# Layer 1's modulation summed on VectorE in layer 0's feed-forward, and the two context units of a head pair apart in layer 1's latent attention

## What is computed

```python
mod = jax.nn.silu(cond) @ lp["w_mod"] + lp["b_mod"]            # (1024) @ (1024, 6144), for 2 conditions
sh1, sc1, g1, sh2, sc2, g2 = jnp.split(mod[:, None, :], 6, axis=-1)
h = _rms(x, lp["norm1_g"]) * (1.0 + sc1) + sh1
z = h @ lp["w_in"]                                             # queries, keys, values and gates of three branches
...
o_a = _attend(q_a, k_a, v_a)                                   # branch B, latent attention, 8 heads
o_d = _attend(q_d0, k_d0, v_all, q_d1, k_d1, lam)              # branch D, differential attention, 4 heads
x = x + g1 * (y @ lp["w_out"])
h2 = _rms(x, lp["norm2_g"]) * (1.0 + sc2) + sh2
x = x + g2 * (jnp.square(jax.nn.relu(h2 @ lp["w_ff1"])) @ lp["w_ff2"])
```

## Time and profile before

| | |
|---|---|
| median of 3 runs | 2543.97 us |
| the profiled execution | 2543.29 us, span 2541.5 us |
| TensorE busy | 2466.6 us (97% of the span) |
| VectorE busy | 1115.3 us (44%) |
| ScalarE busy | 827.5 us (33%) |
| GpSimd busy | 1347.6 us (53%) |
| mean granted TensorE clock | 0.994 of full speed |

### The profile page before, as it was taken

How to read it: one execution, slowest core, us unless ns; L and a number is a source line. 1 busy time by engine, 2 the same in 40 slices (tenths; PEclk the granted TensorE clock), 3 DMA queues, 4 the chain that set the end, 5 groups by cost and what they waited for, 6 DMA issues and landing times.

```text
span 2541.5 us, 41382 instructions
## 1 busy us (share of the span) xinstructions
PE 2466.6 (97%) x17104; PEld 2314.0 (91%) x17104; DVE 1115.3 (44%) x1610; ACT 827.5 (33%) x1517; POOL 1347.6 (53%) x635
## 2 busy tenths in 40 slices
PE   5999999999999999999989999999999999999997
PEld 3989976988999999999979899679889999999997
DVE  5443465434446423132564525653454463222235
ACT  3261355435422302021224423553554132112031
POOL 2646520554566666666656456016455666666664
PEclk8999999999999999999999999999999999999999
DMA  6202235521122222222211122342111222222221
GB/s 270 75 26 76 78 112 181 195 86 50 51 70 73 75 75 75 75 75 75 75 58 59 39 80 78 142 158 79 55 42 62 72 75 75 75 76 75 75 75 58
DMA packets 62619, 214.63 MB, mean 84 GB/s; under 512 B 6816, under 2 KB 11360, under 8 KB 62176
## 3 DMA queue, kind: packets, MB, share of 16 engines
q1 hardware_dynamic: 56160, 202.92, 23.9%
q10 hardware_dynamic: 6272, 9.07, 1.0%
HBM read 207.14 MB, written 4.49 MB: 83 GB/s over the span
## 4 chain that ended last, share of the span: by engine, by line
PE 90%; DVE 4%; ACT 2%; DVEq 1%; issue 1%; DMA 1%; SPq 1%; POOL 0%; POOLq 0%; ACTq 0%
PE big L567 22%; PE big L571 22%; PE big L570 22%; PE four L753 6%; PE big L828 2%; PE big L776 2%; PE four L649 2%; PE four L859 2%; PE four L840 2%; PE four L798 1%; PE big L595 1%; PE big L598 1%; PE big L599 1%; PE four L973 1%; DMA first_mod<-in_first 1%
## 5 line engine op out<-in xcount | busy, mean ns | idle before, releaser
L527 POOL TENSOR_TENSOR w_hi<-raw,cst 128x1024 fp32r<-128x1024 f32 (+1 forms) x286 | 546.4, 1910 | 1044.3 <-PE big L567 835.2
L530 POOL TENSOR_TENSOR w_lo<-raw,w_hi 128x1024 fp32r<-128x1024 f32 (+1 forms) x286 | 734.5, 2568 | 40.8
L567 PE MATMUL big<-act_hi,w_hi 128*128 128x320 f32 x2304 | 716.8, 311 | 1.3 <-DVE act_lo L2214 1.2
L571 PE MATMUL big<-act_hi,w_lo 128*128 128x320 f32 x2304 | 711.8, 309 | 0.0
L570 PE MATMUL big<-act_lo,w_hi 128*128 128x320 f32 x2304 | 711.8, 309 | 0.0
L567 PEld LDWEIGHTS big<-act_hi,w_hi 128*128 128x128 f32 x2304 | 432.5, 188 | 8.9 <-issue 5.6
L570 PEld LDWEIGHTS big<-act_lo,w_hi 128*128 128x128 f32 x2304 | 432.5, 188 | 1.1
L571 PEld LDWEIGHTS big<-act_hi,w_lo 128*128 128x128 f32 x2304 | 432.4, 188 | 0.0
L567 PE MATMUL big<-u_hi,w_hi 128*128 128x320 f32 (+1 forms) x1024 | 319.0, 312 | 1.9 <-DVE u_lo L2233 1.9
L570 PE MATMUL big<-u_lo,w_hi 128*128 128x320 f32 (+1 forms) x1024 | 317.4, 310 | 0.0
L571 PE MATMUL big<-u_hi,w_lo 128*128 128x320 f32 (+1 forms) x1024 | 317.0, 310 | 0.0
(11 more groups left out here) (328 smaller groups left out, 4040.6 us busy)
## 6 DMA issues: line engine op xcount, KB each, us to landing
raw<-in_w SPq DMA_DIRECT2D x366, 512.0 KB, 3.4
first_mod<-in_first SPq DMA_DIRECT2D x16, 512.0 KB, 15.7
x<-in_x ACTq DMA_DIRECT2D x1, 2560.0 KB, 12.8
out_y<-x SPq DMA_DIRECT2D x8, 320.0 KB, 2.6
cst<-in_const ACTq DMA_DIRECT2D x1, 1665.0 KB, 8.9
small<-in_small ACTq DMA_DIRECT2D x2, 437.0 KB, 9.1
out_C<-c_new ACTq DMA_DIRECT2D x2, 258.0 KB
v_d<-in_past ACTq DMA_DIRECT2D x2, 256.0 KB, 3.2
```

Source lines behind the costliest of these rows:

```text
L527: nc.gpsimd.tensor_tensor(w_hi[:, to, 0:n], raw[:, slot, 0:n], ones[:, 0:1].to_broadcast([P, n]), ALU.mult)
L530: nc.gpsimd.tensor_tensor(w_lo[:, to, 0:n], raw[:, slot, 0:n], w_hi[:, to, 0:n].bitcast(f32), ALU.subtract).then_inc(split_ready, 1)
L567: first = mm(ps, wh, ah, start=k == 0, stop=False)
L571: last = mm(ps, wl, ah, start=False, stop=k == nk - 1)
```

## The change

Layer 1's 48 modulation blocks are taken off TensorE. They are loaded in layer 0's feed-forward, one behind each dense block from feed-forward block 3 on. VectorE weighs each one (`weigh`) behind its own work on feed-forward tiles 2 to 49: it reads half of `raw` (512 columns), multiplies by a condition's value on each partition and adds to an accumulator in PSUM (`two`), for two k and two conditions, so four instructions for each block; the last k of each half chunk goes to SBUF (`mod_acc`). TensorE then adds over the partitions of one chunk with eight products against `mod_pick`, in front of tile 8q+11, ScalarE copies that row, TensorE turns it in front of tile 8q+13, and VectorE keeps it behind that tile. The host lays out layer 1's blocks in halves of 512 columns. In layer 1's latent attention the units of a head pair stand in the order `APART`: the context units are fifth and eighth of ten. The values of two units are multiplied once both are there. Layer 0's latent attention is as it was, modulation included.

```diff
+MOD_LEAD = 3
+MOD_FIRST_TILE = 2
+def mod_chunk_at(tile, behind):
+    q, r = divmod(tile - MOD_FIRST_TILE - KD - behind, KD)
+    return q if r == 0 and 0 <= q < MOD_CHUNKS else None
...
 def ring_order():
...
-    dq = FIRST_BLOCK["dq"] + 1
-    out = []
-    for l in range(DEPTH):
-        out += dense(l, 0, dq) + mod(l, MOD_A, MOD_BLOCKS)
-        for m in range(8) if l + 1 < DEPTH else ():
-            out += dense(l, dq + m, dq + m + 1) + mod(l + 1, 2 * m, 2 * m + 2)
-        out += dense(l, dq + (8 if l + 1 < DEPTH else 0), DENSE)
-    return out
+    dq, ff = FIRST_BLOCK["dq"] + 1, FIRST_BLOCK["ff"]
+    out = dense(0, 0, dq) + mod(0, MOD_A, MOD_BLOCKS) + dense(0, dq, ff + MOD_LEAD)
+    for n in range(MOD_BLOCKS):
+        out += dense(0, ff + MOD_LEAD + n, ff + MOD_LEAD + n + 1) + mod(1, n, n + 1)
+    return out + dense(0, ff + MOD_LEAD + MOD_BLOCKS, DENSE) + dense(1, 0, DENSE)
...
+APART = ((0, 0), (0, 1), (1, 0), (1, 1), (LATE, 0), (2, 0), (2, 1), (LATE, 1), (3, 0), (3, 1))
...
+        mod_pick = sb("mod_pick", [P, 2, 32])
...
+        mod_acc = at("mod_acc", [P, 2, 2, BLK], A0 + 41088)
...
+        def latent_units(l):
+            if l == 0:
+                return attention_units(H_A, 2)
+            return [(2 * p + g, t) for p in range(H_A // 2) for t, g in APART]
+        def value_groups(l):
+            units = latent_units(l)
+            pairs = sorted({(h // 2, t) for h, t in units}, key=lambda pt: max(units.index((2 * pt[0] + g, pt[1]))
+                                                                               for g in range(2)))
+            return [(p, t, [units.index((2 * p + g, t)) for g in range(2)]) for p, t in pairs]
+        def values_done(l, i):
+            return 2 * [n for n, (_, _, of) in enumerate(value_groups(l)) if i in of][0] + 2
...
-            def mod_pair(l, m):
-                q, k = divmod(2 * m, KD)
-                if m == 0:
-                    pe.wait_ge(o_copied, (l - 1) * 8 + 8)
-                if k == 0:
-                    pe.wait_ge(row_copied, l * MOD_CHUNKS + q)
-                mod_block(l, KD * q + k, one[0][:, 0:256])
-                mod_block(l, KD * q + k + 1, one[0][:, 0:256])
-                if k == 2 and q:
-                    mod_turn(l, q - 1, one[1][:, 0:256])
+            def mod_sum(q, out):
+                pe.wait_ge(mod_weighted, q + 1)
+                if q:
+                    pe.wait_ge(row_copied, MOD_CHUNKS + q)
+                for g in range(2):
+                    for r in range(4):
+                        last = mm(out[32 * r:32 * r + 32, :], mod_pick[:, g, :],
+                                  mod_acc[:, q % 2, g, 256 * r:256 * r + 256], start=g == 0, stop=g == 1)
+                last.then_inc(mod_summed, 1)
+            def mod_in_ff(tile):
+                q = mod_chunk_at(tile, 1)
+                if q is not None:
+                    mod_sum(q, last_two[:, 0, 0:256])
+                q = mod_chunk_at(tile, 3)
+                if q is not None:
+                    if q:
+                        pe.wait_ge(mod_kept, MOD_CHUNKS + q)
+                    mod_turn(1, q, last_two[:, 1, 0:256])
...
-                    p, t = divmod(j, 5)
+                    p, t, of = groups[j]
                     if j == 0:
                         pe.wait_ge(v_copied, l * 2 + 1)
-                    pe.wait_ge(pT_copied, l * 60 + 2 * (j + 1))
+                    pe.wait_ge(pT_copied, l * 60 + of[1] + 1)
                     if p and t in (0, LATE):
-                        pe.wait_ge(o_copied, l * 8 + 2 * p - (t == 0))
+                        late_first = l > 0
+                        pe.wait_ge(o_copied, l * 8 + 2 * p - ((t == 0) != late_first))
...
-                    if 0 <= i - 2 and i % 2:
-                        if i % 10 == 1:
-                            pe.wait_ge(mod_kept, l * MOD_CHUNKS + 3 + (i - 11) // 10)
-                        values((i - 2) // 2)
+                    for j, (p, t, of) in enumerate(groups):
+                        if of[1] == i - 2:
+                            if i % 10 == 1:
+                                pe.wait_ge(mod_kept, l * MOD_CHUNKS + 3 + (i - 11) // 10)
+                            values(j)
...
-                attend(l, mod_beside(l))
+                attend(l, mod_beside(l) if l == 0 else lambda i: None)
                 for m in range(8):
                     project(l, USE["dq"][m:], FIRST_BLOCK["dq"] + m, 1, KD, act_hi, act_lo)
-                    if l + 1 < DEPTH:
-                        mod_pair(l + 1, m)
-                def turn_second_chunk(b):
-                    if b == 1 and l + 1 < DEPTH:
-                        pe.wait_ge(mod_kept, (l + 1) * MOD_CHUNKS + 1)
-                        mod_turn(l + 1, 1, one[1][:, 0:256])
-                project_tokens(l, USE["dv"], FIRST_BLOCK["dv"], None, turn_second_chunk)
-                if l + 1 < DEPTH:
-                    pe.wait_ge(mod_kept, (l + 1) * MOD_CHUNKS + 2)
+                project_tokens(l, USE["dv"], FIRST_BLOCK["dv"])
                 pe.wait_ge(o_copied, l * 8 + 8)
                 pe.wait_ge(roped, l * 8 + 8)
...
                 for c in range(FF_CHUNKS):
                     block = FIRST_BLOCK["ff"] + 16 * c
                     for m in range(16):
+                        if l + 1 < DEPTH:
+                            mod_in_ff(16 * c + m)
                         if c == 0 and m == 1:
...
                     if i >= 4:
-                        act.wait_ge(o_ready, l * 60 + 2 * (i // 2 - 1))
+                        act.wait_ge(o_ready, l * 60 + values_done(l, i - 4))
                     n = CTX if t == LATE else T
                     f(probT_a[:, i % 4, :, :].rearrange("p c q -> p (c q)")[:, 0:n],
...
             def keep_row(l, c, src):
                 q = l * MOD_CHUNKS + c
-                act.wait_ge(mod_block_used, KD * (q + 1))
+                if l:
+                    act.wait_ge(mod_summed, c + 1)
+                else:
+                    act.wait_ge(mod_block_used, KD * (q + 1))
...
-                    if l + 1 < DEPTH and m == 4:
-                        keep_row(l + 1, 0, one[0][:, 0:256])
...
-                    if l + 1 < DEPTH and m == 7:
-                        keep_row(l + 1, 1, one[0][:, 0:256])
...
                 for c in range(FF_CHUNKS):
-                    for m in range(8):
-                        relu_square(c, m)
-                        round_ff(c, m)
+                    for m in range(16):
+                        if m < 8:
+                            relu_square(c, m)
+                            round_ff(c, m)
+                        q = mod_chunk_at(16 * c + m, 1)
+                        if l + 1 < DEPTH and q is not None:
+                            keep_row(l + 1, q, last_two[:, 0, 0:256])
...
-                    if i >= 4 and i % 2 == 0:
-                        outputs((i - 4) // 2)
+                    for j, (_, _, of) in enumerate(groups):
+                        if of[1] == i - 3:
+                            outputs(j)
...
+            def weigh(n):
+                c, at = divmod(n, KD)
+                half, j = divmod(at, KD // 2)
+                place = PLACE["mod", 1, n]
+                dve.wait_ge(raw_loaded[place % RAW], 16 * (place // RAW + 1))
+                if c >= 2 and at == 0:
+                    dve.wait_ge(mod_summed, c - 1)
+                for k in (2 * j, 2 * j + 1):
+                    src = raw[:, place % RAW, 512 * (k % 2):512 * (k % 2) + 512]
+                    for g in range(2):
+                        acc = two[:, g, :]
+                        out = acc if k < KD - 1 else mod_acc[:, c % 2, g, 512 * half:512 * half + 512]
+                        if k == 0:
+                            last = v.tensor_scalar(out, src, cond[:, k, g:g + 1], None, ALU.mult)
+                        else:
+                            last = v.scalar_tensor_tensor(out, src, cond[:, k, g:g + 1], acc, ALU.mult, ALU.add)
+                    if k % 2:
+                        last.then_inc(mod_block_used, 1)
+                    dve.drain()
+                if at == KD - 1:
+                    dve.drain().then_inc(mod_weighted, 1)
+            def mod_in_ff(tile):
+                if 0 <= tile - MOD_FIRST_TILE < MOD_BLOCKS:
+                    weigh(tile - MOD_FIRST_TILE)
+                q = mod_chunk_at(tile, 3)
+                if q is not None:
+                    if q == 0:
+                        dve.wait_ge(small_loaded, 32)
+                    keep_mod(1, q, FIRST_CHUNKS[q] if q < 2 else q, last_two[:, 1, 0:256])
...
-                keep_mods = mods_beside(l)
+                keep_mods = mods_beside(l) if l == 0 else lambda i: None
...
-                    if l + 1 < DEPTH and m == 6:
-                        dve.wait_ge(small_loaded, (l + 1) * 16 + 16)
-                        keep_mod(l + 1, 0, FIRST_CHUNKS[0], one[1][:, 0:256])
-                if l + 1 < DEPTH:
```

(10 more changed lines are left out.)

20 lines of the change are left out of this document (13 added, 7 removed).

## The result

The change runs in **2530.77 us** (median of 4 runs, 2530.35 to 2532.76) against 2544.23 us before on the same chip (4 runs, 2542.97 to 2544.73): ratio 0.9948, 95% interval 0.9936 to 0.9961. The forecast was 2530.0 us in a range of 2521 to 2539 us, and faster. The profiled execution took 2530.97 us, with a span of 2529.2 us (before: 2541.5) and a granted clock of 0.995.

What follows compares the result with a forecast made beforehand. TensorE was taken to bound the kernel (90% of the chain). -8.86 - 13.7 + 8.9 = -13.7 us from the profiled 2543.29 gave 2529.6, forecast as 2530 us since the runs' median is 0.7 higher; range 2521 to 2539 us.

Steps and rivals of the forecast that it cites:

- Layer 0, dq to dv: Layer 0's dq, dk and dv stages without modulation take layer 1's 84.84 us instead of 93.70, a gain of 8.86 us.
- Layer 1's latent attention: Without its modulation groups and turns on TensorE, this stage takes 91.9 us, a gain of 13.7 us.
- 3.6 + 3.2 + 2.0: Layer 1's attention waits: 0.9 us per pair, 1.6 at start and end each, 1 extra in each of two pairs.
- The rival of waits taking the filler's place: Layer 1's latent attention gains only 3.6 to 6 us because waits replace modulation; total 2538 to 2540 us; chance 0.12.
- Feed-forward: Layer 0's feed-forward: six chunk sums, six turns and their insertions add 8.9 us to TensorE, all on the chain.
- the gap: TensorE in layer 0's feed-forward: each inserted group costs about 0.13 us beyond its length, for 12 insertions 1.6 us.
- VectorE: covered: Layer 0's feed-forward: 192 weighing instructions at 0.71 us, 2.95 us per tile, fit VectorE's spare time and cost nothing.
- The threshold of 4.3 us a block: Layer 0's feed-forward: VectorE cannot keep up from 4.3 us a block (7.09 - 2.8), or 1.07 us an instruction.
- The slower rival: VectorE cannot keep up in the feed-forward: 21 us over, 2551 us, or over 2600 if every instruction is stretched; chance 0.07.
- Loads and GpSimd: Layer 0's feed-forward: 48 more loads of 512 KB through the ring, and GpSimd's work beside them, cost nothing.
- the rival of the late ring: Loads late behind tile 7 of three feed-forward chunks, by 2 us each: total 2536 us; chance 0.05.
- The clock: Granted clock falls to 0.87 in layer 1's latent attention, making it 13 us longer: total 2543 us; chance 0.03.

Runs made afterwards that it cites:

- experiment 4: Changed kernel with head-preparation copies spread over the passes, and the second `four` result buffer awaited only before the first product writing it: 2526.62 us.
- experiment 5: Changed kernel with only the head-preparation copies spread over the passes, a repeat of experiment 3 with the same edit: 2529.2 us.
- experiment 9: Changed kernel with TensorE's sum of each chunk over the partitions done twice in a row, 16 products instead of 8: 2535.36 us.
- experiment 11: Changed kernel with layer 1's 48 modulation blocks multiplied on TensorE, one by one, in layer 0's feed-forward; no VectorE weighing or chunk sums: 2562.53 us.
- experiment 2: Changed kernel with the running sums of the weighing in SBUF instead of PSUM: 2547.06 us.
- experiment 8: Changed kernel with eight weighing instructions a block instead of four, each done twice: 2581.42 us.
- experiment 1: Changed kernel with `APART` undone, so layer 1's context units stand side by side, last in a head pair: 2531.52 us.
- experiment 6: Changed kernel with 84 of the 192 weighing instructions left out, from the second condition's sum: 2531.04 us.
- experiment 7: Changed kernel with six weighing instructions a block instead of four, those of odd k done twice: 2534.31 us.
- experiment 3: Changed kernel with each later head pair's six preparation copies spread over passes of the pair before, in both layers: 2529.71 us.

## Why the prediction was right

- **Layer 0, dq to dv: exact** (-8.86 us). The other layer was the experiment. The wait of 0.84 us stayed as said, and experiment 4 shows that it was removable.
- **Layer 1's latent attention: 92.46 us for 91.9.** TensorE's own work was 83.66 us for 83.1. The wait behind the context unit's scores is 0.85 us for 0.8 in the last two pairs, and 1.25 and 1.12 in the first two, where VectorE also makes the copies. All waits together are 8.8 us, which is what the sum has (3.6 + 3.2 + 2.0), in pieces that miss by about half a microsecond each: 4.8 us in the first two pairs for 5.4, 1.0 in the third for 0.9, and 3.1 in the last for 2.5. That the total fits so closely is partly luck. `APART` gave 0.9 us for 1 to 2. The copies in the early pairs were a real bound: spreading them gains 1.5 us (experiment 5). The rival of waits taking the filler's place fell: 8.8 us of waits against 6.2 before is 2.6 us more, where it needed 10 or more.
- **Feed-forward: +8.52 us for +8.9.** The total was near, in part by luck, since two terms were off in opposite directions: the products 0.85 us instead of 1.00, the gap 0.18 instead of 0.13 (experiment 9). Carried over to single blocks (experiment 11) the same two terms came out 4 to 8 us short in 30.
- **VectorE: covered, as argued.** 0.75 us each for 0.71, no wait. The threshold of 4.3 us a block held as an order of size: 2.9 us cost nothing, 4.4 cost 4.5 us, and 5.8 (experiment 2, four mean instructions) or 5.9 (experiment 8) cost 16.7 and 50.0 us. What it misses is where the cover gives first: the forecast and its rival counted up projection tiles, but all of the new waits with six instructions, and more than half in experiments 2 and 8, are at the chunk sums. Experiments 2 and 8 keep VectorE busy for 398 and 418 of 481 and 515 us. Their growth is 13.2 and 34.2 us of new waits and 3.4 and 15.7 us of TensorE's busy time; why waits and clock differ so much for blocks of nearly the same mean length was not taken apart. The slower rival, with 0.07 in the forecast, was one accumulator in SBUF away.
- **Loads and GpSimd: nothing**, as said; no wait of TensorE goes back to the ring. GpSimd's idle time before its splits (167.4 us) is all ended by TensorE and none of it by a load, so the rival of the late ring fell.
- **The clock: a rival that can come true in small.** In the change it stays at 1.00 in layer 1's latent attention. It fell for about 4 us at the end of the stage in three other executions, which cost 1.5 to 1.6 us and not the 13 us of a whole stage at 0.87 (see the last section).
- **Not predicted:** +0.37 us in layer 0's latent attention. It belongs to the change and not to chance: the change and the seven versions that leave the copies where they were (experiments 1, 2, 6 to 9 and 11) have 106.00 to 106.05 us there. All of it arises at one turn, which waits 0.36 us longer for VectorE's product; that product starts after 0.45 us in which VectorE stood idle and waited for nothing that the profile shows:

```profile
409.53 0.55 DVE L1836 TENSOR_SCALAR prob_a<-prob_a,cols 128x640 f32<-128x640 f32 x1 [0.45 <-issue]
```

  The same product waits for nothing in the kernel before, and has this delay in every other version too. Experiments 3 to 5 come back to 105.7 us by other means, since the spread copies gain 0.35 us. What delays the product stays open.

## What to carry to other kernels

Work put on the bounding engine costs its full time where that engine never waits (experiment 11: 29.8 us, all of it busy time), and less where it fills waits: in layer 1's latent attention 15.9 us of it (TensorE busy 99.51 us before, 83.66 after) were worth 13.2. Moving it to an engine with slack pays if each instruction stays under a threshold that is worked out from the pace of the bounding engine, and if the latest due time (here each chunk's last block) is checked by itself. Where the accumulator lies can decide more than the operation: beside GpSimd's splits the same instruction took 0.75 us with its running sum in PSUM and on the average 1.45 us with it in SBUF. A mean can hide two kinds: half of the latter took 0.75 us as well. Take the price of an inserted group from a difference of two stages or two kernels, since a row of the chain can already hold part of the gap, and price the size of group that you will insert: a single block cost 0.33 us beyond its products, where the six sums and six turns had cost 0.18 us each.

## What the hardware showed that I had not expected

- **The clock after short waits.** In experiment 3 the granted clock fell to 0.57 over 4 us right behind waits of 1.0 and 0.9 us, and cost 1.6 us; in experiments 4 and 5, and in the change, the same waits left it at 1.00. Of the ten traces with these two waits three show the fall, always at this place: experiments 3, 8 and 11. In experiment 11, where dq begins at 1716.36 us, latent attention takes 93.52 us and dq to dv 85.15, together 1.5 us more than in the change:

```profile
1711.00:1719.00 8.00, 6.16 (x45) 5.39 (x45) 2.26 (x4) 3.06 (x5) 1.86 (x1) 0.79 0.01 2
```

What decides in which execution it falls stays open.
- **`tensor_scalar` beside GpSimd** takes 748 ns with its result in PSUM, and 1059 or 1705 ns on the average with it in SBUF (experiments 2 and 6), though its input is in SBUF in all three. In experiment 2 the twelve that meet no split take 474 to 490 ns and the longest of the others 2634: with its result in SBUF it is faster alone and slower in company. I had allowed for a stretch of the first products, and there was none. The Trainium skill, "VectorE: DVE Perf Modes", section "Why PSUM operands drop a tier", says that an operand in PSUM keeps an instruction out of the mode that takes both ports; the 743 to 757 ns beside splits, against 474 to 490 ns without and up to 2634 with them where the result lies in SBUF, agree with it.
